# Adding up the forget-gate quarters later, and putting the last pair of recurrent gates one projection later, in a fused two-block kernel

## The reference

```
def second_block(x, ...):
    for l in range(DEPTH_2):
        x = x + 0.5 * swiglu(rms_norm_2(x, ffn1_norm[l]), ...)
        h = rms_norm_2(x, mix_norm[l])
        proj = h @ w_in[l] + b_in[l]
        q, k, v, f_logit, xr, gr, g_attn, g_rnn = jnp.split(proj, SPLIT_POINTS, axis=-1)
        q = rms_norm_2(q.reshape(B, S, N_HEADS, HEAD_DIM), q_norm[l])
        k = rms_norm_2(k.reshape(B, S, N_HEADS, HEAD_DIM), k_norm[l])
        log_f = jax.nn.log_sigmoid(f_logit.astype(jnp.float32))
        y_attn = forgetting_attention(q, k, v, log_f) @ w_o_attn[l]
        xr = causal_depthwise_conv(xr, conv_w[l], conv_b[l])
        yr = rg_lru(xr, lru_w_a[l], ..., lru_lambda[l]) * jax.nn.gelu(gr)
        y_rnn = yr @ w_o_rnn[l]
        merged = jax.nn.sigmoid(g_attn) * y_attn + jax.nn.sigmoid(g_rnn) * y_rnn
        x = x + merged @ w_out[l]
        x = x + 0.5 * swiglu(rms_norm_2(x, ffn2_norm[l]), ...)

def rg_lru(x, w_a, b_a, w_x, b_x, lam):      # w_a, w_x: 16 blocks of 64 x 64
    r = sigmoid(block_diag_linear(x, w_a, b_a)); i = sigmoid(block_diag_linear(x, w_x, b_x))
    log_a = -8 * r * softplus(-lam)
    a, u = exp(log_a), sqrt(-expm1(2.0 * log_a)) * (i * x)
    h_t = a_t * h_{t-1} + u_t                # an associative scan over the 512 positions
```

## Time and profile before

| | us |
|---|---|
| median of 3 runs (3305.65 to 3306.15) | 3305.78 |
| the profiled execution | 3305.81 |
| its span | 3304.1 |
| PE busy | 3288.7 (100%) |
| DVE, ACT, POOL busy | 2273.0, 1532.7, 2197.9 |

### The profile page before, as it was taken

How to read it: one execution, slowest core, us unless ns; L and a number is a source line. 1 busy time by engine, 2 the same in 40 slices (tenths; PEclk the granted TensorE clock), 3 DMA queues, 4 the chain that set the end, 5 groups by cost and what they waited for, 6 DMA issues and landing times.

```text
span 3304.1 us, 54409 instructions
## 1 busy us (share of the span) xinstructions
PE 3288.7 (100%) x18310; PEld 2811.7 (85%) x18310; DVE 2273.0 (69%) x3503; ACT 1532.7 (46%) x2141; POOL 2197.9 (67%) x2139
## 2 busy tenths in 40 slices
PE   9999999999999999999999999999999999999999
PEld 5888778899889997788888899889987888888998
DVE  8887685988877878714435888778878334247887
ACT  4365664443443336735544333533347445534333
POOL 6443445877769886553356888689875544468896
PEclk9999999999999999999999999999999999999999
DMA  6221453322232223332223322233223222223232
GB/s 225 89 71 65 166 179 115 119 97 99 89 115 96 102 89 102 102 122 65 75 89 108 115 101 103 77 115 114 93 86 115 90 102 71 83 95 109 102 109 101
DMA packets 94488, 343.40 MB, mean 104 GB/s; under 512 B 10609, under 2 KB 11249, under 8 KB 93954
## 3 DMA queue, kind: packets, MB, share of 16 engines
q1 hardware_dynamic: 86978, 312.11, 27.5%
q10 hardware_dynamic: 7360, 29.29, 2.8%
HBM read 335.03 MB, written 2.13 MB: 102 GB/s over the span
## 4 chain that ended last, share of the span: by engine, by line
PE 85%; DVE 5%; POOL 4%; DVEq 2%; issue 2%; ACT 1%; DMA 0%; ACTq 0%; SPq 0%; POOLq 0%
PE ps L689 25%; PE ps L691 25%; PE ps L690 25%; POOL w_lo L635 3%; POOL t_lo L635 1%; PE ps L856 1%; PE ps L857 1%; PE ps L858 1%; PE ps L1391 1%; PE ps L1373 1%; PE ps L938 1%; PE ps L884 1%; DVE arena L2765 1%; PE ps L1382 1%; DVEq L2787 0%
## 5 line engine op out<-in xcount | busy, mean ns | idle before, releaser
L635 POOL TENSOR_TENSOR w_lo<-raw,w_hi 128x256 fp32r<-128x256 f32 (+1 forms) x1468 | 1306.3, 920 | 906.8 <-ACT w_hi L1479 905.1
L689 PE MATMUL ps<-a_hi,w_lo 128*128 128x512 f32 (+1 forms) x2728 | 1020.6, 374 | 1.1 <-POOL w_lo L635 0.7
L691 PE MATMUL ps<-a_hi,w_hi 128*128 128x512 f32 (+1 forms) x2728 | 1006.1, 369 | 0.0
L690 PE MATMUL ps<-a_lo,w_hi 128*128 128x512 f32 (+1 forms) x2728 | 1005.4, 369 | 0.0
L635 POOL TENSOR_TENSOR w_lo<-arena,w_hi 128x512 fp32r<-128x512 f32 x514 | 780.4, 1544 | 170.9 <-ACT w_hi L2078 114.6
L689 PEld LDWEIGHTS ps<-a_hi,w_lo 128*128 128x128 f32 x2728 | 513.4, 188 | 100.4 <-issue 18.0
L691 PEld LDWEIGHTS ps<-a_hi,w_hi 128*128 128x128 f32 x2728 | 512.4, 188 | 87.8
L690 PEld LDWEIGHTS ps<-a_lo,w_hi 128*128 128x128 f32 x2728 | 512.8, 188 | 80.8 <-issue 0.5
L1479 ACT ACTIVATE w_hi<-raw 128x1024 fp32r<-128x1024 f32 x321 | 336.6, 1053 | 324.5 <-PE ps L691 305.2
L689 PE MATMUL ps<-b_hi,w_lo 128*128 128x512 f32 (+1 forms) x1052 | 390.1, 371 | 0.6 <-POOL w_lo L635 0.2
L2078 ACT ACTIVATE w_hi<-arena 128x1024 fp32r<-128x1024 f32 x192 | 203.7, 1061 | 398.0 <-PE ps L691 398.0
(11 more groups left out here) (365 smaller groups left out, 4982.1 us busy)
## 6 DMA issues: line engine op xcount, KB each, us to landing
raw<-in_stream SPq DMA_DIRECT2D x419, 512.0 KB, 3.3
arena<-in_stream SPq DMA_DIRECT2D x148, 512.0 KB, 3.3
arena<-in_mod_w ACTq DMA_DIRECT2D x32, 512.0 KB, 4.2
arena<-in_mod_w SPq DMA_DIRECT2D x16, 512.0 KB, 11.6
arena<-arena ACTq DMA_DIRECT2D x16, 256.0 KB, 3.7
arena<-cum_rows ACTq DMA_DIRECT2D x2, 2048.0 KB, 9.6
xres<-in_x_t SPq DMA_DIRECT2D x4, 512.0 KB, 5.3
arena<-in_first SPq DMA_DIRECT2D x8, 256.0 KB, 11.8
```

The costliest lines, as they stand in the source:

```text
L635: last = pool.tensor_tensor(to[:, at], of[:, at], hi[:, at].bitcast(F32), ALU.subtract)
L689: pe.matmul(out, lo, x_hi, start=start, stop=False)
L690: pe.matmul(out, hi, x_lo, start=False, stop=False)
L691: return pe.matmul(out, hi, x_hi, start=False, stop=stop)
```

## The change

In PE's program `forget_total` leaves its place behind the first fresh projections and is called as `beside(7)` of the first group, behind its fourth projection; it gets a wait for the scans of all four pairs, since its bank may be one that pair 3's gates used. The gates of pair 3 come behind the first of two branch-gate projections (`sgate`) and no longer ahead of both. ACT's and DVE's programs follow: ACT evacuates the first `sgate` tile before `recurrent_gates(3)`, and DVE runs `forget_logits` in the first group.

```
             def forget_total():
                 bank = bank_v()
+                pe.wait_ge(lru_scanned, c.scan.at(0))
                 pe.wait_ge(dve_evacuated, quads_read)
...
                 project_fresh(bank_a(), bank_v())
-                forget_total()
                 project(bank_a())
                 lru_gates(1)
                 project(bank_a())
...
                 lru_gates(2)
                 units_of(bank_a)
+                project(bank_a())
                 lru_gates(3)
-                gates()
-
-                queries_keys_values(0, lambda n: None)
+                project(bank_a())
+
+                queries_keys_values(0, lambda n: forget_total() if n == 7 else None)
...
                 recurrent_gelu(0, 1)
                 pass_v()
-                pass_v()
-                gelu_in_place(1, 1, behind=1)
+                gelu_in_place(1, 1)
                 turn_halves(1)
...
                 recurrent_root(2)
-                recurrent_gates(3)
                 need(act, dve_evacuated, c.dve.at(0))
                 evacuate(sgate[:, 0, :], ACT.Sigmoid, bias=par(PAR2, "b_gn", 0))
+                recurrent_gates(3)
                 tick()
                 evacuate(sgate[:, 1, :], ACT.Sigmoid, bias=par(PAR2, "b_gn", 1))
...
                 def beside_first(n):
                     if n == 2:
                         recurrent_out(3)
+                    if n == 7:
+                        pass_v()
...
                 dve.tensor_copy(gr[:, 1, 1, :], y).then_inc(dve_evacuated, 1)
-                forget_logits()
                 recurrence(0)
...
-                queries_keys_values(0, lambda n: None)
+                queries_keys_values(0, lambda n: forget_logits() if n == 7 else None)
                 forget_sums()
```

## The result

The changed kernel took 3315.21 us (median of 9 runs, 3314.69 to 3315.91) against 3305.73 (9 runs, 3305.46 to 3306.31). The ratio is 1.0028, with a 95% interval of 1.0018 to 1.0038: 9.5 us slower. The forecast was 3313.4 (range 3309.5 to 3316.5) and "slower by over 0.2%".

A forecast was written before the change was run, and what follows sets the result against it. PE bounds the kernel, busy 3288.7 of 3304.1 us. First layer 2.35 + 1.1, second 3.0 + 1.1: 7.55 us slower than 3305.81, so 3313.4 us (range 3309.5 to 3316.5; forecast's own 3311.5 to 3315).

The forecast's parts named there:

- Steps 1 to 3: Up to pair 3's gates: removed waits return as waits for pair 1's DMA (1.2 us) and ACT's banks (third unit 1.0).
- step 2: Behind pair 1's gates, a unit waits for ACT's bank; PE 0.82 us early in first layer, second at the same instants.
- Step 4: ACT and DVE chain behind pair 3's gates: second statistics product 2.35 us later in the first layer, 3.0 in the second.
- 12.24 us at their old lengths: From pair 3's root's end to the inverse norm, ACT and DVE alternate without a gap; links counted at old lengths.
- The bound named for this: In step 4's chain: if DVE and POOL disturb each other less, up to 1 us per layer comes back.
- Both statistics products wait for DVE and ACT: Sign on PE behind pair 3: statistics products wait for DVE and ACT, 0.6 and 0.9 us.
- Step 5: Forget product in its new place: costs its 1.1 us in each layer, its new wait costs nothing, nothing queues.
- rival by POOL: POOL's subtraction and DVE's products slow each other by a third, 1.4 us per layer: 3316.2 us; chance 0.1.
- The hidden pair: ACT and DVE close the 2.9 us before the statistics, hiding pair 3's lateness: 3307.3 us; chance 0.15.
- The faster one: The removed waits come back in full, 3.6 us: 3302.2 us; chance 0.05.
- A pause behind the load: ACT stands still 1.28 us behind the added table load in each layer: 3316.0 us; chance 0.05.

The follow-up runs named there:

- forget move alone: Kernel before with only the forget product moved, pair 3's gates ahead of both branch-gate units as before: 3307.34 us (1.0004).
- convolution first on the changed kernel: Changed kernel with pair 3's second input evacuated ahead of pair 1's output and its convolution ahead of pair 1's low part: 3313.06 us (1.0022).
- POOL's work first: Changed kernel with ACT's rounding of the second query's weights, and with it POOL's subtraction, ahead of pair 3's gates: 3314.4 us (1.0026).
- fewer loads: Changed kernel with Identity for the sigmoid on the first two branch-gate tiles, two table loads fewer per layer: 3312.34 us (1.0019).
- gates move alone: Kernel before with only pair 3's gates one unit later, the forget product in its old place: 3313.69 us (1.0024).

## Why the prediction was right, and by how much it was off

**Steps 1 to 3, to the start of pair 3's gates: right.** In the first layer, counted from pair 0's gates, the forecast and the trace are: pair 1's gates 19.7 and 19.33, the unit that waits for the bank 38.41 and 38.42, the third unit 63.41 and 63.40, pair 3's gates 69.04 and 69.07. The removed waits went into a wait for pair 1's DMA (0.84; forecast 1.2), for the bank (0.60), and for the bank again at the third unit (0.83). The forget move alone shows the first two, and the convolution first on the changed kernel shows the cause of the third. One reading was off by little: the last packet in the first DMA row stands in slot 22 of 40 and not 19, so at 1313.05. In the second layer the waits were 1.04, 0.66 and 0.78, and pair 3's gates started 69.33 behind the start, 0.25 later than "the same instants" of step 2.

**Step 4, the chain: right in its cause, its size too small.** The gates block on ACT ended 77.81 behind the start, forecast 77.73; the root 84.17, forecast 84.1. Then came "12.24 us at their old lengths", and that term was 12.90, because DVE's products ran beside POOL's subtraction and finished behind the root (0.49 of the 0.66 us; the other 0.17 is a longer first step of the split square, 0.73 for 0.56). It was 12.90 in the second layer too, and 12.20 where POOL had finished. The inverse norm was at 97.07, forecast 96.3. PE came 0.23 behind that, and not 0.06 as before, through POOL's wait of 2.08 (forecast 1.3) and the slow clock. So step 4 gave 2.35 and 3.0 us, and they were 3.3 and 4.2. The bound named for this, DVE and POOL disturbing each other, was put on the side of a gain, and it was a loss. The run with POOL's work first and the one with fewer loads show that the chain is what holds the time: whatever made PE wait less for POOL gave back a part only.

**"Both statistics products wait for DVE and ACT": wrong for this kernel, true beside it.** In the changed kernel they had no wait. PE was late by itself, by POOL and the clock; where the clock held, 0.38 and 0.69 stood there.

**Step 5, the moved product: 1.17 for 1.1.** From the third statistics product to the one in the values it was 7.39 us (6.22 before). Counted from the second one to the end of the group it is 1.08 and 1.06 in the two layers. Nothing queued behind it.

**The sum.** 7.55 forecast, 9.5 measured. In the traces step 4 gave 0.9 and 1.1 us more than forecast: the link of 12.90 gave 0.66 in each layer, PE's own lateness 0.17 in each, and a root that came later than counted 0.1 and 0.3. So the time lies 0.2 us above the forecast's own range (3311.5 to 3315) and inside the range from 3309.5 to 3316.5 only: the mechanism was the forecast one, and part of the rival by POOL came on top of it.

**The rivals.** The hidden pair is out: the chain ends later than counted, not sooner. The faster one is out too. That by POOL came nearest: 5.22 is 0.8 more than before, about half of what it assumed, and the chain became 0.66 longer in each layer. A pause behind the load is not in any row.

## What to carry to other kernels

When a wait is to be removed, find what stands right behind it on the other engines before counting it: the wait of the forget product, that of pair 3's gates and, with POOL's work first, that for `w_lo` all came back as waits for another resource. Here ACT met PE with 0.06 us to spare, so moving the gates a unit later cost the whole delay of the chain behind them, and undoing one link of it gave back only what the next link left. A moved rounding or subtraction also moves the load that it frees; look at what transfer it then meets.

## What the runs showed of the hardware

TensorE's granted clock fell to its lower level (0.50, 1.2 GHz) behind waits of 2.0 to 2.1 us of an otherwise busy PE, but not each time. It fell in both layers of the changed kernel, in the second of the gates move alone, and in the first of the kernel with POOL's work first and of the changed kernel with the convolution first. It held behind waits of 2.08, 1.99 and 2.07 us in the other layer of these three. Each of these is read from one execution, and when it falls and when it holds stays open. It didn't fall at a fixed distance: within 0.4 us of the restart in the changed kernel and the gates move alone, 1.2 and 1.4 us behind it in the other two. Behind the shorter waits of these stages, up to 1.3 us and once 1.69, it stayed at 1.00. Where it fell, some eight matmuls stood 0.2 us further apart. What that cost hung on what stood behind: 0.13 and 0.15 us where PE would have waited for the chain anyway (gates move alone, convolution first), 0.8 with POOL's work first, where the slow matmuls came behind PE's wait for the chain.

DVE's product of two 128x1024 operands took 1.23 us alone and 1.50 to 1.60 beside POOL's subtraction in the changed kernel. POOL's subtraction of a unit took 2.83 us where DVE rests (at 1398.28 in the trace of before), 4.44 in the earlier trace rows and 5.22 in the changed kernel, both beside DVE's products of tiles of `arena`. Not all of DVE's work slows it: at 1340.90 in the trace of before it took 2.82 us while DVE was busy for 2.75 of them with a product and a scan that read one operand from `ps`.
